# A state-space recurrence whose decay products move from GpSimd to VectorE

## The chip, the cores and the metric

The kernel runs on one core of a Trainium2 chip, as one launch. A core has a matrix engine (TensorE, "PE" in the profile, with its weight loads as "PEld"), VectorE ("DVE"), ScalarE ("ACT"), GpSimd ("POOL") and SyncE ("SP"), each with an instruction queue of its own that runs in order. They share the on-chip memory SBUF. TensorE writes to PSUM, here used as eight banks of 128x512 float32. The metric is the device time of one execution in microseconds (us), the median of several runs.

## The reference, cut to what matters

Two transformer-like blocks run one after the other on 512 tokens of width 1024. The second block has three branches, and one of them is a state-space model (16 heads of width 64, state size 128) that is scanned forward and backward over the sequence in chunks of 128 positions. What is computed per chunk is this:

```python
def ssd_scan(xh, dt, a_coef, bm, cm, h0, want_y):
    ...
    xdt = (xh.astype(f32) * dt[..., None]).reshape(b, nc, q, G, hg, P)
    acs = jnp.cumsum((dt * a_coef.astype(f32)).reshape(b, nc, q, G, hg), axis=2)
    decay_end = jnp.exp(acs[:, :, -1:] - acs)
    states = jnp.einsum('bcjgn,bcjghp->bcghpn', bc, xdt * decay_end[..., None])
    chunk_decay = jnp.exp(acs[:, :, -1])
    def step(h, inp):
        st, dec = inp
        return h * dec[..., None, None] + st, h
    ...
    lmat = jnp.exp(jnp.where(tri[:, :, None, None], seg, -jnp.inf))
    cb = jnp.einsum('bcign,bcjgn->bcijg', cc, bc)
    y_diag = jnp.einsum('bcijgh,bcjghp->bcighp', cb[..., None] * lmat, xdt)
    y_off = jnp.einsum('bcign,bcghpn->bcighp', cc, h_in) * jnp.exp(acs)[..., None]
```

The change touches `cb[..., None] * lmat`, the product of the C-B scores (one 128x128 matrix for each of two groups of heads) with the decays (one 128x128 matrix for each of 16 heads).

## The kernel before

The kernel is written out for each engine by hand: one function per engine and stage, with semaphores between them and no scheduler. The order of the calls is the order of each engine's queue.

The recurrence is `pe_ssm`, `dve_ssm`, `act_ssm` and `pool_ssm`. `ssm_units()` lists twelve chunks: two of the context, then four of the sequence, forward; then two of the context and four of the sequence, backward. The eight chunks of the sequence (`OWN_UNITS`) also yield output; they are called chunk 1 to chunk 8 here, 1 to 4 forward and 5 to 8 backward. Between chunk 4 and chunk 5 lie the two backward context chunks, which only update the state.

What each engine does for one of chunks 1 to 8, in the order of its queue:

- **TensorE**: the old state's part of the output (C times state, two banks, after `ssm_h`); the state's update (B times `xw`, two banks, after `ssm_x`); for the next chunk the C-B scores (one bank) and four banks of decay sums, in `pe_ssm_decays`; then for each of the two groups, after `ssm_probs`, eight heads' products of probabilities (in `decay`) with `xdt`, one bank each. Chunk 8 has no next chunk. Behind it stands `pe_ssm_out`, a projection of 128 matmul records that needs nothing from the recurrence but its turn in the queue.
- **VectorE**: `xw` and `xdt` (128x1024 each, through the helper `tt`, whose operations all carry line 2687); then `ssm_x`; the old state's part scaled (L2715), in the backward direction with an added sum into y (another L2687); the state times its decay (L2687) and plus its update (L2727), for both groups; `ssm_h`; the C-B scores of the next chunk, masked into `cb` (L2665, `dve_ssm_cb`); and the two sums of the group outputs into y (L2737), each followed by `ssm_y`.
- **ScalarE**: for each group, 8 activations on the decay sums (L2791) and one exponential over 128x1024 (L2795), into one of three buffers `decay`. The buffer of three groups earlier must be free (`ssm_y`). Then it raises `ssm_exp`.
- **GpSimd**: for each group, after `ssm_exp` and (once a chunk) `ssm_cb`, the product of the decays with the scores, 128x1024, in place (L2775); then `ssm_probs`.

`decay` has two buffers in the tensor `scratch` and the third in `slots_of_units`. `cb` has two buffers. `to_dve` rotates over four PSUM banks, which VectorE must free, and `to_act` over four others.

Of the kernel before, what the change touches and what calls it, by code (L numbers as in the profile page):

```python
# [10 lines left out]
ALU = mybir.AluOpType  # L11
# [3 lines left out]
P = 128  # L15
# [264 lines left out]
def build(nc, a, table, where, out):  # L280

    ctx = ExitStack()
    with ctx:
# [3 lines left out]
        def sem(name):  # L287
            return ctx.enter_context(nc.semaphore(name))

        def signal(name):  # L290
            return Signal(sem(name))
# [30 lines left out]
        def part(at, *shape):  # L322

            n = int(np.prod(shape))
            assert at + n <= SCRATCH, (at, shape)
            v = scratch[:, at:at + n]
            if len(shape) == 2:
                v = v.rearrange("p (a b) -> p a b", b=shape[1])
            if len(shape) == 3:
                v = v.rearrange("p (a b c) -> p a b c", b=shape[1], c=shape[2])  # L330
            return v

        def con(name, width=None):
            at, n = where[name]
            return const[:, at:at + (width or n)]
# [25 lines left out]
        dve_done = sem("dve_done")  # L361
        pool_done = sem("pool_done")
# [2017 lines left out]
        decay = [*(part(SSM_TMP + i * 1024, 8, P) for i in range(2)), sel.rearrange("p a t s -> p (a t) s")]  # L2380
        cb = [part(SSM_TMP + 2048, 2, P), part(SSM_TMP + 4864, 2, P)]
# [10 lines left out]
        xs_ready = signal("xs_ready")  # L2392
        ssm_x = signal("ssm_x")
        acs_turned = signal("acs_turned")
        ssm_cb = signal("ssm_cb")
        ssm_y = signal("ssm_y")
        ssm_exp = signal("ssm_exp")
        ssm_probs = signal("ssm_probs")
# [206 lines left out]
        OWN_UNITS = [(d, c) for d, c in ssm_units() if c < TT]  # L2605
# [56 lines left out]
        def dve_ssm_cb(dve, i):  # L2662
            dve.wait_ge(to_dve.full, to_dve.next_full())
            bank = to_dve.take()
            dve.tensor_tensor(cb[i % 2], bank[:, 0:256].rearrange("p (g i) -> p g i", g=2),  # L2665
                              con("upper" if OWN_UNITS[i][0] == 0 else "lower").rearrange("p (g i) -> p g i", g=1)
                              .broadcast_to([P, 2, P]), ALU.mult).then_inc(to_dve.free, 1)
            dve.wait_ge(to_dve.free, to_dve.own_reads())
            dve.sem_inc(ssm_cb.sem, 1)

        def dve_acs_rows(dve, step):
            dve.tensor_copy(acs_own, acs[:, :, 0:64]).then_inc(dve_done, 1)
# [13 lines left out]
        def dve_ssm(dve, step):  # L2686
# [3 lines left out]
            n_own = 0  # L2690
# [4 lines left out]
            for d, c in ssm_units():  # L2695
                own = c < TT
                xs = heads(xs_tok[:, c, :] if own else ctx_xs[:, c - TT, :])
                tt(heads(xw), xs, over(head_cols(w_end, d, c), SSM_P), ALU.mult).then_inc(dve_done, 1)
                dve.wait_ge(dve_done, step.next())
                if own:  # L2700
                    tt(heads(xdt), xs, over(head_cols(d_t, d, c), SSM_P), ALU.mult).then_inc(dve_done, 1)
                    dve.wait_ge(dve_done, step.next())
                dve.sem_inc(ssm_x.sem, 1)
                y_g = lambda g: y_tok[:, c, g * 512:(g + 1) * 512].rearrange("p (h x) -> p h x", x=SSM_P)
                if own:
                    if n_own == 0:
                        dve_ssm_cb(dve, 0)
                    n_own += 1
                    if c == (0 if d == 0 else TT - 1):
                        dve.sem_inc(ssm_h.sem, 1)  # L2710
                    for g in range(2):
                        dve.wait_ge(to_dve.full, to_dve.next_full())
                        bank = to_dve.take()
                        dst = y_g(g) if d == 0 else y_part.rearrange("p (h x) -> p h x", x=SSM_P)
                        dve.tensor_tensor(dst, bank[:, :].rearrange("p (h x) -> p h x", x=SSM_P),  # L2715
                                          over(head_cols(e_acs, d, c, g), SSM_P), ALU.mult).then_inc(to_dve.free, 1)
                        dve.wait_ge(to_dve.free, to_dve.own_reads())
                        if d == 1:
                            tt(y_g(g), y_g(g), dst, ALU.add).then_inc(dve_done, 1)
                            dve.wait_ge(dve_done, step.next())  # L2720
                for g in range(2):
                    h = h_state[d][:, 8 * g:8 * g + 8, :]
                    tt(h, h, over(head_cols(e_tot, d, c, g), SSM_P), ALU.mult).then_inc(dve_done, 1)
                    dve.wait_ge(dve_done, step.next())
                    dve.wait_ge(to_dve.full, to_dve.next_full())
                    bank = to_dve.take()
                    dve.tensor_tensor(h, h, bank[:, :].rearrange("p (h x) -> p h x", x=SSM_P), ALU.add).then_inc(to_dve.free, 1)  # L2727
                    dve.wait_ge(to_dve.free, to_dve.own_reads())
                if own:
                    if c != (TT - 1 if d == 0 else 0):  # L2730
                        dve.sem_inc(ssm_h.sem, 1)
                    if n_own < len(OWN_UNITS):
                        dve_ssm_cb(dve, n_own)
                    for g in range(2):
                        dve.wait_ge(to_dve.full, to_dve.next_full())
                        bank = to_dve.take()
                        dve.tensor_tensor(y_g(g), y_g(g), bank[:, :].rearrange("p (h x) -> p h x", x=SSM_P), ALU.add)\  # L2737
                           .then_inc(to_dve.free, 1)
                        dve.wait_ge(to_dve.free, to_dve.own_reads())
                        dve.sem_inc(ssm_y.sem, 1)  # L2740
# [25 lines left out]
        y_rms = part(SSM_TMP + 2048, TT)  # L2766
        ys_t = freed[0].rearrange("p (m t) -> p m t", t=T)

        def pool_ssm(pool, step):
            for i in range(len(OWN_UNITS)):  # L2770
                pool.wait_ge(ssm_cb.sem, ssm_cb.next(pool))
                for g in range(2):
                    own = decay[(2 * i + g) % 3]
                    pool.wait_ge(ssm_exp.sem, ssm_exp.next(pool))
                    pool.tensor_tensor(own, own, cb[i % 2][:, g:g + 1, :].broadcast_to([P, 8, P]), ALU.mult)\  # L2775
                        .then_inc(pool_done, 1)
                    pool.wait_ge(pool_done, step.next())
                    pool.sem_inc(ssm_probs.sem, 1)

        def act_ssm(act, step):  # L2780
            for i, (d, c) in enumerate(OWN_UNITS):
# [630 lines left out]
        @block.gpsimd  # L3412
        def _(pool):
            step = Order()
            pool_s5_steps(pool)
            pool_row_loads(pool)
            pool_s5_loads(pool)
            pool_s5(pool, step)
            pool_moe_loads(pool)
            pool_bias(pool, step)  # L3420
            pool_store_tokens(pool)
            pool_moe(pool, step)
            pool_ssm(pool, step)
            pool_rope_load(pool)

        @block.tensor
# [117 lines left out]
```

## Time and profile before

| | us |
|---|---|
| median of 3 runs | 3664.16 |
| lowest and highest | 3656.54, 3665.57 |
| the profiled execution | 3668.7 |
| its span, first to last instruction | 3666.9 |
| TensorE busy in the span | 3200.5 (87%) |
| VectorE busy | 1231.0 (34%) |
| ScalarE busy | 521.5 (14%) |
| GpSimd busy | 269.6 (7%) |

The eight chunks of the recurrence run from about 2209.7 us to 2326 us of the span. Times in the rows count from the start of the span. A row of the timeline gives the start, the duration of the merged instructions, engine, source line, what is written and read, how many instructions were merged, and in brackets the engine's idle time before them and what ended it. A merged row shows the shape of its first instruction. A float32 matmul into a bank leaves two records, so that two banks show as x4.

### The profile page before, as it was taken

Reading aid. Unit: us, or ns where it says so; the run is one execution under the profiler, and the core shown is the slowest. Engines: PE = TensorE matmul, PEld = TensorE weight load, DVE = VectorE, ACT = ScalarE, POOL = GpSimd, SP = SyncE. Lnnn points to the kernel's source line nnn. Section 1 sums busy time; section 2 is a strip of 40 time slices with the busy share of each in tenths; the row PEclk is TensorE's granted clock in tenths of the full one; section 3 lists DMA queues with packets and bytes.
Section 4 is the critical chain, followed back from the end, with each engine's and each line's share of the span. In section 5 each row is a group of like instructions: output and inputs, shape, how many; then the busy total and the mean of one; then the engine's idle time right before and its main releaser. Section 6 shows DMA issues by size and latency. Waiting matters only on the chain.

```text
span 3666.9 us, 33500 instructions
## 1 busy us (share of the span) xinstructions
PE 3200.5 (87%) x13492; PEld 1532.1 (42%) x13493; DVE 1231.0 (34%) x2047; ACT 521.5 (14%) x981; POOL 269.6 (7%) x352
## 2 busy tenths in 40 slices
PE   4894758699999999999994888978868999899998
PEld 2352223444443333333332554446636444344444
DVE  3126990523223232323233236514254001212201
ACT  1211001200110000000001214213133000100000
POOL 0005650200000000000000003100000000000000
PEclk8896779699999999999997798986879999999999
DMA  9511410289999999999993110010000222121210
GB/s 294 179 69 55 149 69 23 88 321 330 327 334 333 356 352 360 352 355 353 359 360 134 46 35 1 24 52 1 24 23 1 69 81 92 46 90 59 75 63 23
DMA packets 287682, 582.43 MB, mean 159 GB/s; under 512 B 7953, under 2 KB 12492, under 8 KB 287500
## 3 DMA queue, kind: packets, MB, share of 16 engines
q1 hardware_dynamic: 281184, 561.20, 42.7%
q0 software_dynamic: 5072, 15.80, 1.9%
q10 hardware_dynamic: 1276, 3.29, 0.2%
q8 instruction: 110, 1.80, 0.2%
q14 instruction: 40, 0.33, 0.0%
HBM read 576.08 MB, written 4.19 MB: 158 GB/s over the span
## 4 chain that ended last, share of the span: by engine, by line
PE 77%; DVE 15%; ACT 3%; issue 2%; SPq 1%; POOL 1%; DMA 1%; ACTq 1%; DVEq 0%; PEldq 0%; POOLq 0%
PE psum_all L211 74%; DVE scratch L1197 4%; PE psum_all L219 3%; DVE hidden L2039 2%; SPq L188 1%; DVE scratch L1221 1%; DVE scratch L3102 1%; DVE scratch L2687 1%; ACTq L566 1%; DVE scratch L1214 1%; ACT scratch L3164 1%; DMA panel<-in_ada_w 1%; DVE scratch L2983 1%; ACT hidden L424 0%; DVE scratch L832 0%
## 5 line engine op out<-in xcount | busy, mean ns | idle before, releaser
L211 PE MATMUL psum_all<-panel,scratch 128*64 128x512 f32 (+3 forms) x5568 | 977.5, 507 | 1.4 <-ACTq L1814 0.8
L211 PE MATMUL psum_all<-hidden,panel 128*128 128x512 f32 (+1 forms) x1808 | 795.2, 601 | 31.3 <-ACT hidden L424 20.9
L211 PEld LDWEIGHTS psum_all<-hidden,panel 128*128 128x128 f32 (+1 forms) x1808 | 346.5, 192 | 471.3 <-issue 440.9
L211 PEld LDWEIGHTS psum_all<-panel,scratch 128*64 128x64 f32 (+2 forms) x5568 | 333.8, 131 | 472.7 <-issue 426.1
L211 PE MATMUL psum_all<-scratch 128*128 128x64 f32 (+8 forms) x1512 | 371.3, 442 | 132.5 <-DVEq L1235 82.5
L211 PEld LDWEIGHTS psum_all<-scratch 128*128 128x128 f32 (+2 forms) x1512 | 232.6, 235 | 242.5 <-DVEq L1235 97.9
L2039 DVE TENSOR_TENSOR hidden<-hidden,psum_all 128x512 f32<-128x512 f32 x264 | 169.6, 684 | 290.9 <-PE psum_all L211 290.9
L211 PE MATMUL psum_all<-scratch,panel 128*128 128x512 f32 (+1 forms) x672 | 250.5, 531 | 2.0 <-DVE resid L3289 1.0
L219 PE MATMUL psum_all<-const,scratch 128*128 128x128 f32 (+4 forms) x954 | 152.2, 299 | 114.4 <-DMA scratch<-in_s_lambda_im 32.9
L219 PEld LDWEIGHTS psum_all<-const,scratch 128*128 128x128 f32 (+4 forms) x954 | 111.0, 157 | 215.1 <-issue 109.5
L211 PE MATMUL psum_all<-scratch,const 128*128 128x512 f32 (+5 forms) x308 | 120.0, 534 | 83.1 <-ACT scratch L415 32.1
L211 PEld LDWEIGHTS psum_all<-scratch,panel 128*128 128x128 f32 x672 | 127.5, 190 | 127.5 <-issue 119.6
L2029 DVE SCALAR_TENSOR_TENSOR y_low<-psum_all,scratch,y_high 128x512 fp32r<-128x512 f32 (+1 forms) x49 | 33.6, 686 | 271.5 <-ACT y_high L2001 271.5
L211 PE MATMUL psum_all<-tokens_r,y_high 64*128 64x512 f32 (+2 forms) x360 | 97.0, 496 | 28.2 <-DVE hidden L2039 26.6
L211 PE MATMUL psum_all<-panel,hidden 128*128 128x512 f32 (+2 forms) x384 | 111.4, 455 | 10.4 <-ACT hidden L424 10.4
L211 PEld LDWEIGHTS psum_all<-scratch,const 128*128 128x128 f32 x308 | 59.0, 234 | 135.2 <-issue 68.2
L1812 ACT ACTIVATE scratch<-psum_all 128x512 f32<-128x512 f32 (+1 forms) x49 | 26.7, 545 | 617.8 <-PE psum_all L219 617.8
L1425 POOL DMA_INDIRECT scratch<-token_rows,scratch x33 | 30.8, 934 | 1115.5 <-DVEq L1771 1115.5
L211 PE MATMUL psum_all<-panel 128*128 128x512 f32 x256 | 110.5, 592 | 1.7 <-DVEq L3280 1.7
L1197 DVE TENSOR_TENSOR scratch<-scratch 128x512 f32<-128x512 f32 x128 | 104.9, 840 | 4.6
L2019 DVE TENSOR_SCALAR scratch<-psum_all 128x512 f32<-128x512 f32 (+1 forms) x49 | 30.7, 626 | 218.6 <-PE psum_all L211 218.6
L2539 DVE TENSOR_SCALAR scratch<-psum_all,cols 128x512 f32<-128x512 f32 (+1 forms) x44 | 33.0, 750 | 193.2 <-PE psum_all L211 193.2
(323 smaller groups left out, 2299.8 us busy)
## 6 DMA issues: line engine op xcount, KB each, us to landing
panel<-in_exp_w_gu SPq DMA_DIRECT2D x132, 2048.0 KB, 11.8
panel<-in_exp_w_down SPq DMA_DIRECT2D x66, 2048.0 KB, 14.3
panel<-in_w_in SPq DMA_DIRECT2D x17, 2048.0 KB, 8.3
panel<-in_ada_w SPq DMA_DIRECT2D x12, 2048.0 KB, 20.1
panel<-in_w_mod SPq DMA_DIRECT2D x12, 2048.0 KB, 7.9
panel<-in_ffn_w_gate SPq DMA_DIRECT2D x5, 2048.0 KB, 7.8
panel<-in_ffn_w_up SPq DMA_DIRECT2D x5, 2048.0 KB, 7.7
panel<-in_w_out SPq DMA_DIRECT2D x4, 2048.0 KB, 7.8
```

The source lines that it names most:

```text
L188: sp.dma_start(dst, src.rearrange("(k p) c -> p k c", p=P)).then_inc(self.loaded[s], 16)
L211: ins = self.pe.matmul(out, lhsT, rhs, start=start, stop=stop)
L219: return self.pe.transpose(out, in_, ident)
L566: act.dma_start(rows[at:at + n, tile_no, :], flat(name).rearrange("(r c) -> r c", c=P))\
L1197: tt = lambda o, x, y, op: dve.tensor_tensor(o, x, y, op)
L1214: dve.tensor_tensor_scan(z_re, mag, w1, 0.0, ALU.mult, ALU.add).then_inc(dve_done, 1)
L1221: dve.tensor_tensor_scan(z_im, mag, w3, 0.0, ALU.mult, ALU.add).then_inc(dve_done, 1)
L2039: dve.tensor_tensor(hidden[:, m, :], hidden[:, m, :], moe_y(no)[:, :], ALU.add).then_inc(shares_free, 1)
L2687: tt = lambda o, x, y, op: dve.tensor_tensor(o, x, y, op)
L2983: dve.reciprocal(nrm_std[:, 0:n], nrm_std[:, 0:n]).then_inc(dve_done, 1)
L3102: dve.tensor_reduce(tmp_max[:, 0:1], pair[:, 512 - w:768], AX_X, ALU.max).then_inc(dve_done, 1)
L3164: act.activation(p_sb[u % 2][:, 0:w + CTX], att_pairs[u % 2][:, 512 - w:768], ACT.Exp, bias=neg_max[n % 2][:, h:h + 1], scale=HD ** -0.5, ...
```

## The change

The function `pool_ssm` and its call are gone, with the semaphore `ssm_cb`. A function `dve_ssm_probs` makes the same two products on VectorE. `dve_ssm` calls it in each of chunks 1 to 8 behind the state's updates and `ssm_h`, ahead of `dve_ssm_cb` for the next chunk and ahead of the two sums into y.

```diff
@@
-        ssm_cb = signal("ssm_cb")
@@
             dve.wait_ge(to_dve.free, to_dve.own_reads())
-            dve.sem_inc(ssm_cb.sem, 1)
@@
                     if c != (TT - 1 if d == 0 else 0):
                         dve.sem_inc(ssm_h.sem, 1)
+                    dve_ssm_probs(dve, step, n_own - 1)
                     if n_own < len(OWN_UNITS):
                         dve_ssm_cb(dve, n_own)
@@
-        def pool_ssm(pool, step):
-            for i in range(len(OWN_UNITS)):
-                pool.wait_ge(ssm_cb.sem, ssm_cb.next(pool))
-                for g in range(2):
-                    own = decay[(2 * i + g) % 3]
-                    pool.wait_ge(ssm_exp.sem, ssm_exp.next(pool))
-                    pool.tensor_tensor(own, own, cb[i % 2][:, g:g + 1, :].broadcast_to([P, 8, P]), ALU.mult)\
-                        .then_inc(pool_done, 1)
-                    pool.wait_ge(pool_done, step.next())
-                    pool.sem_inc(ssm_probs.sem, 1)
+        def dve_ssm_probs(dve, step, i):
+            for g in range(2):
+                own = decay[(2 * i + g) % 3]
+                dve.wait_ge(ssm_exp.sem, ssm_exp.next(dve))
+                dve.tensor_tensor(own, own, cb[i % 2][:, g:g + 1, :].broadcast_to([P, 8, P]), ALU.mult).then_inc(dve_done, 1)
+                dve.wait_ge(dve_done, step.next())
+                dve.sem_inc(ssm_probs.sem, 1)
@@
-            pool_ssm(pool, step)
```

VectorE's queue in chunk 3 (forward), before. The lines are those named above, from `xw` and `xdt` to the two sums into y:

```order
L2687 TENSOR_TENSOR scratch<-panel,scratch 128x1024 x2
L2715 TENSOR_TENSOR panel<-psum_all,scratch 128x512 x2
L2687 TENSOR_TENSOR scratch<-scratch 128x512
L2727 TENSOR_TENSOR scratch<-scratch,psum_all 128x512
L2687 TENSOR_TENSOR scratch<-scratch 128x512
L2727 TENSOR_TENSOR scratch<-scratch,psum_all 128x512
L2665 TENSOR_TENSOR scratch<-psum_all,const 128x256
L2737 TENSOR_TENSOR panel<-panel,psum_all 128x512 x2
```

The same place after the change. Line numbers there are one or two lower, and the products stand at L2772:

```order
L2685 TENSOR_TENSOR scratch<-panel,scratch 128x1024 x2
L2713 TENSOR_TENSOR panel<-psum_all,scratch 128x512 x2
L2685 TENSOR_TENSOR scratch<-scratch 128x512
L2725 TENSOR_TENSOR scratch<-scratch,psum_all 128x512
L2685 TENSOR_TENSOR scratch<-scratch 128x512
L2725 TENSOR_TENSOR scratch<-scratch,psum_all 128x512
L2772 TENSOR_TENSOR scratch<-scratch 128x1024
L2772 TENSOR_TENSOR slots_of_units<-slots_of_units,scratch 128x1024
L2664 TENSOR_TENSOR scratch<-psum_all,const 128x256
L2736 TENSOR_TENSOR panel<-panel,psum_all 128x512 x2
```

Two operations of 128x1024 now stand between the last state update and the next chunk's scores.

VectorE's queue in chunk 8, the last (backward), after the change, from the state's decays and updates on; before, the two rows of L2772 were absent and the rest was the same:

```order
L2685 TENSOR_TENSOR scratch<-scratch 128x512
L2725 TENSOR_TENSOR scratch<-scratch,psum_all 128x512
L2685 TENSOR_TENSOR scratch<-scratch 128x512
L2725 TENSOR_TENSOR scratch<-scratch,psum_all 128x512
L2772 TENSOR_TENSOR slots_of_units<-slots_of_units,scratch 128x1024
L2772 TENSOR_TENSOR scratch<-scratch 128x1024
L2736 TENSOR_TENSOR panel<-panel,psum_all 128x512 x2
L2685 TENSOR_TENSOR panel<-panel,row_vectors 128x1024
```

Nothing moved on TensorE. Its queue in chunk 8 and behind it, with its waits, is the same before and after: old state, update, the two groups behind `ssm_probs`, and the projection:

```order
L211 MATMUL psum_all<-scratch 128x512 [waits dve_banks_free,ssm_h]
L211 MATMUL psum_all<-scratch 128x512 [waits dve_banks_free]
L211 MATMUL psum_all<-scratch 128x512 [waits dve_banks_free,ssm_x]
L211 MATMUL psum_all<-scratch 128x512 [waits dve_banks_free]
L211 MATMUL psum_all<-scratch,slots_of_units 128x64 [waits dve_banks_free,ssm_probs]
L211 MATMUL psum_all<-scratch,slots_of_units 128x64 x7
L211 MATMUL psum_all<-scratch 128x64 [waits dve_banks_free,ssm_probs]
L211 MATMUL psum_all<-scratch 128x64 x7
L211 MATMUL psum_all<-panel,hidden 128x512 [waits act_banks_free,panel2_0_loaded]
```

What moved is who raises `ssm_probs` for the two waits there: GpSimd before, VectorE after its state updates now.

## Rows read from the trace of the kernel before

**Rows 1.** The page: busy us (share of the span of 3666.9 us) by engine.

```profile
PE 3200.5 (87%) x13492; PEld 1532.1 (42%) x13493; DVE 1231.0 (34%) x2047; ACT 521.5 (14%) x981; POOL 269.6 (7%) x352
```

**Rows 2.** The chain that ended last (start, us, what), around chunks 6 and 7.

```profile
2294.99 9.39 PE psum_all L211 x48
...
2307.84 9.39 PE psum_all L211 x48
```

**Rows 3.** The same chain from chunk 8 on.

```profile
2320.69 60.50 PE psum_all L211 x164
```

**Rows 4.** GpSimd's products in `scratch`, by line: duration ns min/median/max, first and last start.

```profile
L2775 POOL TENSOR_TENSOR scratch<-scratch x11: 2349/2361/3155, 2214.9 to 2319.7; 128x1024 f32<-128x1024 f32 x11
```

**Rows 5.** VectorE by line and shape, 2195 to 2332 us: busy us, mean ns | idle before.

```profile
L2687 DVE TENSOR_TENSOR scratch<-scratch 128x512 f32<-128x512 f32 x24 | 22.1, 919 | 1.3
L2687 DVE TENSOR_TENSOR scratch<-panel,scratch 128x1024 f32<-128x1024 f32 x16 | 19.6, 1225 | 1.2
...
L2687 DVE TENSOR_TENSOR panel<-panel,scratch 128x512 f32<-128x512 f32 x8 | 9.1, 1140 | 0.3
```

**Rows 6.** Timeline of VectorE in chunk 3, forward.

```profile
2237.76 2.48 DVE L2687 TENSOR_TENSOR scratch<-panel,scratch 128x1024 f32<-128x1024 f32 x2
...
2241.84 1.16 DVE L2687 TENSOR_TENSOR scratch<-scratch 128x512 f32<-128x512 f32 x1
...
2244.49 0.69 DVE L2727 TENSOR_TENSOR scratch<-scratch,psum_all 128x512 f32<-128x512 f32 x1
2245.32 0.42 DVE L2665 TENSOR_TENSOR scratch<-psum_all,const 128x256 f32<-128x256 f32 x1
```

**Rows 7.** Timeline of TensorE in chunk 3.

```profile
2240.36 2.43 PE L211 MATMUL psum_all<-scratch 128*128 128x512 f32 x8 [1.70 <-DVEq L2703]
...
2246.06 1.89 PE L211 MATMUL psum_all<-scratch 128*128 128x64 f32 x16
```

**Rows 8.** Timeline of GpSimd: a product in chunk 3, one in the context chunks.

```profile
2239.30 3.15 POOL L2775 TENSOR_TENSOR slots_of_units<-slots_of_units,scratch 128x1024 f32<-128x1024 f32 x1 [2.60 <-ACTq L2797]
...
2265.01 2.72 POOL L2775 TENSOR_TENSOR scratch<-scratch 128x1024 f32<-128x1024 f32 x1 [2.59 <-ACTq L2797]
```

**Rows 9.** Timeline of VectorE in chunk 6, backward.

```profile
2295.75 1.89 DVE L2687 TENSOR_TENSOR panel<-panel,scratch 128x512 f32<-128x512 f32 x1
...
2301.29 0.69 DVE L2727 TENSOR_TENSOR scratch<-scratch,psum_all 128x512 f32<-128x512 f32 x1
```

**Rows 10.** Timeline of TensorE in chunk 6, the first group's products.

```profile
2300.69 1.90 PE L211 MATMUL psum_all<-scratch 128*128 128x64 f32 x16
```

**Rows 11.** Timeline of VectorE in the first backward context chunk.

```profile
2266.76 1.52 DVE L2687 TENSOR_TENSOR scratch<-scratch 128x512 f32<-128x512 f32 x1
```

**Rows 12.** Timeline of VectorE in chunk 8.

```profile
2321.45 1.88 DVE L2687 TENSOR_TENSOR panel<-panel,scratch 128x512 f32<-128x512 f32 x1
...
2326.99 0.69 DVE L2727 TENSOR_TENSOR scratch<-scratch,psum_all 128x512 f32<-128x512 f32 x1
```

**Rows 13.** Timeline of TensorE: chunk 8's first group, then the projection behind it.

```profile
2322.51 1.90 PE L211 MATMUL psum_all<-scratch,slots_of_units 128*128 128x64 f32 x16
...
2326.03 55.15 PE L211 MATMUL psum_all<-panel,hidden 128*128 128x512 f32 x128
```

**Rows 14.** Timeline of TensorE behind two of its idle stretches.

```profile
2270.37 2.08 PE L211 MATMUL psum_all<-scratch 128*128 128x512 f32 x2 [3.59 <-DVEq L2703]
...
2403.66 8.86 PE L211 MATMUL psum_all<-hidden,panel 128*128 128x512 f32 x13 [5.67 <-issue]
```

**Rows 15.** Stretches: length, PE, PEld, DVE, ACT, POOL busy, PE clock, DMA, GB/s.

```profile
2270.00:2273.00 3.00, 2.63 (x3) 1.18 (x4) 1.40 (x3) 0.00 (x0) 0.00 (x0) 0.50 0.00 0
2273.00:2276.00 3.00, 0.77 (x2) 0.00 (x0) 2.86 (x5) 0.00 (x0) 0.00 (x0) 0.96 0.01 3
...
2405.00:2408.00 3.00, 3.00 (x4) 1.01 (x3) 0.00 (x0) 0.00 (x0) 0.00 (x0) 0.50 0.00 0
2408.00:2411.00 3.00, 3.00 (x6) 1.26 (x5) 0.00 (x0) 0.00 (x0) 0.00 (x0) 0.70 0.00 0
```

## Prediction, written before the change was run

> **What bounds the kernel now.** I read the page first, then the chain that ended last, then the timelines of the engines in the recurrence. The page shows TensorE busy 87% of a span of 3666.9 us, VectorE 34% and GpSimd 7% [rows 1], but these are averages over many stages, and the change touches about 117 us of them. The chain shows what ends last there. In chunk 6 it is an unbroken 9.39 us of TensorE, the next chunk's begins 12.85 us later, and the 3.46 us between are VectorE: the second sum into y, then xw and xdt [rows 2]. From chunk 8 on the chain stays on TensorE for 60.50 us, through the projection behind the recurrence [rows 3]. GpSimd is on the chain nowhere in the stage: a product takes it 2.35 to 3.16 us [rows 4], but it is done before TensorE asks for it. So the question isn't whether VectorE makes the product faster. It is whether VectorE gets to it before TensorE does, since it now stands behind VectorE's own state updates.
>
> **What a product costs on VectorE.** The trace has no product of decays and scores on VectorE. The nearest rows are xw and xdt: same size of 128x1024 float32, two SBUF inputs, one of them broadcast, 1.23 us each [rows 5]. The other end is what GpSimd needs for the very same operands, 2.36 us [rows 4]. I take 1.24 us, because the engine, the size and the kind of operands agree, and keep 2.36 for the range. Nothing in the shape suggests less than 1.23.
>
> **What goes away.** The sixteen products leave GpSimd, about 40 us of it; by itself that is worth nothing, as it is off the chain. But some of VectorE's operations get shorter. An operation of 128x512 on two SBUF inputs takes 0.69 us when it is left alone, and 1.16 us in chunk 3 [rows 6], 1.89 in chunk 6 [rows 9], 1.52 in the context chunk [rows 11]. Each long one ends 0.55 us after a GpSimd product ends: 2243.00 against 2242.45, and 2268.28 against 2267.73 [rows 6, 8, 11]. So it had stood waiting for that product. Over the stage this makes 22.1 - 24 x 0.69 = 5.5 us and 9.1 - 8 x 0.69 = 3.6 us, 9.1 us together [rows 5]. The Trainium skill has this as a rule (SBUF — State Buffer, section Who interferes with whom): a VectorE instruction with two SBUF inputs and a GpSimd instruction that reads SBUF exclude one another, and the later one waits out the first. The trace agrees. With the change these waits end, and the question is where on the chain they lay.
>
> **Forward chunks.** In chunk 3 the last state update ends at 2244.49 + 0.69 = 2245.18 [rows 6]. Without the wait (1.16 - 0.69 = 0.47) it ends at 2244.71. From such an end to the next operation behind a semaphore is 0.14 us (2245.18 to 2245.32 [rows 6]), then the product's 1.24, and from the end of xdt to TensorE's start is 0.12 us (2240.24 to 2240.36 [rows 6, 7]). TensorE can begin the first group at 2244.71 + 0.14 + 1.24 + 0.12 = 2246.21. Before, it began at 2246.06 [rows 7]. So 0.15 us is lost. The second product is ready 1.4 us later, and TensorE is busy with the first group for 1.9 us, so it costs nothing. The scores for the next chunk (L2665) and the sums into y queue behind the products; the scores' bank is needed only by the next chunk's old-state matmul, which waits for the second group anyway, and the sums wait for TensorE. Chunks 2, 3 and 4 have the same pattern: 3 x 0.15 = 0.45 us. In chunks 1 and 5 TensorE does the old state's matmuls behind xw instead of ahead of it, and so asks for the first group later; the same working puts the first product ready 0.3 and 0.8 us ahead of need there: nothing.
>
> **Context chunk.** The wait in the first backward context chunk lies on the chain, which is VectorE there: 1.52 - 0.69 = 0.83 us gained [rows 11].
>
> **Backward chunks 6 and 7.** VectorE has two more sums into y ahead of the state updates. The last update ended at 2301.98, and without the wait (1.89 - 0.69 = 1.20) at 2300.78 [rows 9]. Plus 0.14 + 1.24 + 0.12 gives 2302.28, against 2300.69 before [rows 10]: 1.59 us each, 3.2 for two. Had the wait not gone it would be 2.79 each.
>
> **Chunk 8.** Here TensorE has no work for a next chunk, so it wants the first group 3.4 us earlier relative to VectorE, at 2322.51 [rows 13]. VectorE's last update ended at 2327.68, without the wait (1.88 - 0.69) at 2326.49 [rows 12]. Plus 0.14 + 1.24 + 0.12: 2327.99, so 5.5 us lost. Nothing hides this: the projection's 128 records stand behind these groups in TensorE's queue, run at 55.15 us without a pause [rows 13], and the chain goes through them [rows 3]. VectorE's own tail behind chunk 8 moves too, but it runs beside that projection.
>
> **TensorE's clock.** This stall is a TensorE idle of about 5.3 us, and there is none so long in the stage before. After an idle of 3.59 us the granted clock was 0.50, that is 1.2 GHz, and back up by about 2273.2: some 2.9 us of work at the lower level [rows 14, 15]. After an idle of 5.67 us it was at 0.50 until about 2409.8 (0.70 over 2408 to 2411), 6.1 us of work [rows 14, 15]. Work at 1.2 GHz loses half its time: 1.4 and 3.1 us, and 0 if the clock holds. I take 2.3 us, the middle of the two that were seen. The context chunks pass through such a fall before as well; with 0.83 us less idle there it may come out up to 1.4 us better, which I leave to the range.
>
> **The sum.** 0.45 - 0.83 + 3.2 + 5.5 + 2.3 = 10.6 us. Against the profiled execution, 3668.7 us, that is 3679.3. That execution lies 4.5 us above the median of 3664.16, and the runs span 3656.54 to 3665.57, so the sum goes onto the median: 3674.8 us, +0.29%. A measurement of this kernel can tell about 0.3%, 11 us, from no change; the forecast lies just inside that.
>
> **The rivals.**
> - **The clock gives way more often** (slower). In chunks 6 and 7 TensorE gets a second idle of 1.5 us beside the 1.70 us that it has (as in [rows 7]). If the clock falls in each of them as it did after 5.67 us, that is 2 x 3.1 = 6.2 us more: 3681. It decides from the point where two short idles count as one long; against it, the clock stays up in these chunks before.
> - **The product is slow on VectorE** (slower). At 2.36 us, each first product is 1.12 later, on the path in chunks 2, 3, 4, 6, 7, 8, and partly in 1 and 5 (6 x 1.12 + 0.8 + 0.3 = 7.8); the second product then comes 2.5 us after the first, 0.8 more than TensorE's group lasts, 8 x 0.8 = 6.4. Together 14.2: 3689. Against it stand the 1.23 us of like operations.
> - **The last stall is taken back** (same). If what follows chunk 8 were waiting for something else, a panel or ScalarE, the 5.5 + 2.3 would vanish: 3667. Against it, the chain is TensorE alone for 60.50 us.
> - **The lifted waits win** (faster). This is the rule of the skill carried to its end. If all 9.1 us that VectorE stood waiting came off the path, and the products were covered, as GpSimd's were: 3664.2 - 9.1 = 3655. Against it, only 0.83 us of them lie on the chain before; the rest serve to bring the products forward.
>
> **How the numbers follow.** The forecast gets 0.53, and its variant without the clock's fall (3672.5) 0.14; the clock rival 0.12, the slow product 0.06, the absorbed stall 0.10, the lifted waits 0.05. The forecast lies next to the bound of 0.3%, and a median of few runs moves by some us, so it gives 0.27 to slower and 0.26 to same; its variant 0.12 to same and 0.02 to slower. Slower: 0.27 + 0.02 + 0.11 + 0.06 = 0.46. Same: 0.26 + 0.12 + 0.01 + 0.10 + 0.02 = 0.51. Faster: 0.03. The range runs from 3665, just under the absorbed stall, to 3684, past the clock rival with the runs' scatter. It leaves out the slow product and the lifted waits.
>
> **What would show it.** In the profile of the changed kernel: VectorE's products at 1.24 us; no VectorE operation of 128x512 above 0.7 us in the stage; chunks 2 to 4 a period of 13.0 us, chunks 6 and 7 one of 14.4 (12.85 before); TensorE idle about 5.3 us ahead of chunk 8's first group, with `ssm_probs` as what ends it, and a granted clock of 0.50 behind. If the exponentials rather than the products ended a wait, if the period stayed at 12.85 in chunks 6 and 7, or if the projection still began within 1 us of its old distance to chunk 8's xdt, the reasoning would be wrong.

## The result, and the profile after

The changed kernel took 3674.21 us in the median of 9 runs (3670.46 to 3677.91), against 3665.54 us of the kernel before in 9 runs. The ratio is 1.0024, with a 95% interval of 1.0014 to 1.0035: slower by 8.7 us, next to the forecast of 3674.8, and inside what was to be called no change (0.3%). Run again beside the experiments it came out at 3678.09 against 3667.29, 1.0035 (1.0022 to 1.0047), just outside; both intervals hold 0.3%. The size lies between 0.24% and 0.35%, as far as is known.

The page of the kernel after, busy time by engine, answers [rows 1]:

```profile
PE 3200.6 (87%) x13492; PEld 1531.3 (42%) x13493; DVE 1241.6 (34%) x2063; ACT 521.6 (14%) x981; POOL 226.8 (6%) x336
```

GpSimd lost 16 instructions and 42.8 us. VectorE gained 16 and only 10.6 us, since 19.6 us of products came in and some 9 us of waiting went out. The products by line (duration ns min/median/max, first and last start) answer [rows 4]:

```profile
L2772 DVE TENSOR_TENSOR scratch<-scratch x11: 1225/1225/1227, 2217.7 to 2330.6; 128x1024 f32<-128x1024 f32 x11
L2772 DVE TENSOR_TENSOR slots_of_units<-slots_of_units,scratch x5: 1224/1225/1226, 2230.9 to 2329.2; 128x1024 f32<-128x1024 f32 x5
```

All sixteen took what xw takes, 1.23 us, half of GpSimd's 2.36.

VectorE's timeline in chunk 3 of the kernel after answers [rows 6]: the operation that had taken 1.16 us takes 0.69, and the two products stand behind the last state update, 0.15 us after it.

```profile
2241.01 0.69 DVE L2685 TENSOR_TENSOR scratch<-scratch 128x512 f32<-128x512 f32 x1
...
2243.18 0.69 DVE L2725 TENSOR_TENSOR scratch<-scratch,psum_all 128x512 f32<-128x512 f32 x1
2244.02 1.23 DVE L2772 TENSOR_TENSOR scratch<-scratch 128x1024 f32<-128x1024 f32 x1
2245.39 1.23 DVE L2772 TENSOR_TENSOR slots_of_units<-slots_of_units,scratch 128x1024 f32<-128x1024 f32 x1
```

TensorE's timeline in chunks 6, 7 and 8 of the kernel after answers [rows 10, 13]. The first three rows begin with a first group, and the bracket names VectorE's signal behind the product (line 2774) as what TensorE waited for. The last two are chunk 8's second group and the projection, whose row ends with the window shown:

```profile
2300.10 2.00 PE L211 MATMUL psum_all<-scratch 128*128 128x64 f32 x16 [1.41 <-DVEq L2774]
...
2314.64 10.77 PE L211 MATMUL psum_all<-scratch 128*128 128x64 f32 x40 [1.42 <-DVEq L2774]
2330.53 3.67 PE L211 MATMUL psum_all<-scratch,slots_of_units 128*128 128x64 f32 x16 [5.13 <-DVEq L2774]
2334.00 3.62 PE L211 MATMUL psum_all<-scratch 128*128 128x64 f32 x16
2337.41 7.80 PE L211 MATMUL psum_all<-panel,hidden 128*128 128x512 f32 x14
```

The stalls are near those of the forecast (1.5 and 5.3): 1.4 us in chunks 6 and 7, 5.1 in chunk 8. But the groups of chunk 8 took 3.67 and 3.62 us instead of 1.90 each [rows 13], at half the clock. The stretches of 3 us of the kernel after (columns as in [rows 15]) show the clock down in chunk 7 and again behind chunk 8's stall, where it had stood at 1.00 before:

```profile
2316.00:2319.00 3.00, 3.00 (x19) 3.00 (x19) 1.11 (x2) 1.47 (x6) 0.00 (x0) 0.61 0.00 0
2319.00:2322.00 3.00, 3.00 (x8) 1.81 (x8) 1.91 (x2) 2.87 (x5) 0.00 (x0) 0.50 0.00 0
...
2331.00:2334.00 3.00, 3.00 (x17) 3.00 (x16) 0.79 (x1) 0.00 (x0) 0.00 (x0) 0.50 0.00 0
...
2337.00:2340.00 3.00, 3.00 (x6) 1.53 (x7) 2.16 (x3) 0.00 (x0) 0.00 (x0) 0.50 0.00 0
2340.00:2343.00 3.00, 3.00 (x8) 1.38 (x7) 2.93 (x3) 0.00 (x0) 0.00 (x0) 0.90 0.00 0
```

From chunk 1's xw to the end of the projection the kernel before took 171.5 us and the one after 185.4: 13.9 us more, while the whole grew by 8.7 in the median and the span of the profiled execution by 5.9. Chunk 1's xw began 1.0 us earlier (2208.72 against 2209.68), in code that nobody touched; over all traces it lies between 2206.8 and 2211.5. The rest of the difference is behind the projection. The chain of the kernel after, start and duration of three pieces: the first attention's input projection, the second's, and the feed-forward's first long piece.

```profile
2416.55 51.71 PE psum_all L211 x192
...
2621.04 49.99 PE psum_all L211 x192
2835.94 276.41 PE psum_all L211 x640
```

The same of the kernel before:

```profile
2403.66 51.80 PE psum_all L211 x192
...
2612.16 49.79 PE psum_all L211 x192
2830.00 276.44 PE psum_all L211 x640
```

The first attention took 204.5 us after and 208.5 before, the second 214.9 and 217.8. Neither was touched. From the feed-forward to the end it is 836.9 us in both.

The 2.9 us of the second attention have one place. It repeats a group of 20 matmul records, which take 2.83 us at almost every place in both chains; only the one that starts 195 us into this attention differs. First the kernel before, then the kernel after:

```profile
2807.03 5.37 PE psum_all L211 x20
```

```profile
2815.51 2.83 PE psum_all L211 x20
```

Over 2808 to 2811 us the granted clock was 0.50 in the kernel before, and in the kernel after it was 1.00 over 2815 to 2818. So the kernel before had a fall of the clock there that the kernel after did not have.

### The profile page after: what moved, and what is told of

Same layout as the page of the kernel before. It is cut to its first block, busy times and chain, and to the rows that moved or that the text cites. A ratio compares the mean times of both kernels' runs of the same rounds, so it can differ in the third digit from the quotient of the medians.

```text
span 3672.8 us, 33491 instructions
## 1 busy us (share of the span) xinstructions
PE 3200.6 (87%) x13492; PEld 1531.3 (42%) x13493; DVE 1241.6 (34%) x2063; ACT 521.6 (14%) x981; POOL 226.8 (6%) x336
## 4 chain that ended last, share of the span: by engine, by line
PE 76%; DVE 15%; ACT 3%; issue 2%; SPq 1%; POOL 1%; ACTq 1%; DMA 1%; DVEq 0%; PEldq 0%; POOLq 0%
PE psum_all L211 73%; DVE scratch L1197 4%; PE psum_all L219 3%; DVE hidden L2039 2%; SPq L188 1%; DVE scratch L1221 1%; DVE scratch L2685 1%; DVE scratch L3098 1%; ACTq L566 1%; DVE scratch L1214 1%; ACT scratch L3160 1%; DMA panel<-in_ada_w 1%; DVE scratch L2979 1%; ACT hidden L424 0%; DVE scratch L832 0%
## 5 line engine op out<-in xcount | busy, mean ns | idle before, releaser
L211 PE MATMUL psum_all<-panel,hidden 128*128 128x512 f32 (+2 forms) x384 | 112.9, 459 | 10.4 <-ACT hidden L424 10.4
```

The costliest lines, as they stand in the source:

```text
L211: ins = self.pe.matmul(out, lhsT, rhs, start=start, stop=stop)
```

## The experiments

The table reads every trace at the same places. "Stage" is chunk 1's xw to the end of the projection; "6 and 7" are the periods from xw to xw of these chunks; the attention columns go from each input projection's start to the next of the three pieces above. All in us of one profiled execution; the last two columns are the median and the ratio to the kernel before, timed beside it, with its interval. The medians were taken in four rounds, in which the kernel before had 3665.54 (before and after), 3667.29 (e1 to e4), 3665.99 (e5 to e8) and 3666.26 us (e9 to e12), so kernels of different rounds are compared by their ratios. In e7 and e8 xw stands elsewhere in the queue, and no period is given.

| kernel | stage | 6 and 7 | attention 1, 2 | median | ratio |
|---|---|---|---|---|---|
| before | 171.5 | 12.85, 12.85 | 208.5, 217.8 | 3665.54 | |
| after | 185.4 | 14.53, 16.01 | 204.5, 214.9 | 3674.21 | 1.0024 (1.0014 to 1.0035) |
| e1, after again | 185.4 | 14.53, 15.99 | 197.9, 214.8 | 3678.09 | 1.0035 (1.0022 to 1.0047) |
| e2, chunk 8 on GpSimd | 183.2 | 16.72, 16.43 | 204.6, 219.9 | 3680.1 | 1.0036 (1.0024 to 1.0048) |
| e3, only chunk 8 on VectorE | 181.9 | 12.85, 12.85 | 208.2, 214.8 | 3674.7 | 1.0023 (1.0014 to 1.0031) |
| e4, chunk 8's idle filled | 180.6 | 14.53, 16.00 | 209.0, 214.9 | 3678.62 | 1.0028 (1.0016 to 1.0039) |
| e5, products early | 185.2 | 14.65, 14.67 | 204.6, 215.0 | 3677.57 | 1.0032 (1.0020 to 1.0045) |
| e6, no product | 169.4 | 12.85, 12.85 | 206.9, 217.7 | 3666.42 | 1.0001 (0.9992 to 1.0010) |
| e7, xw ahead, GpSimd | 181.1 | | 212.0, 214.9 | 3675.94 | 1.0024 (1.0015 to 1.0033) |
| e8, xw ahead, VectorE | 177.8 | | 205.0, 215.0 | 3669.6 | 1.0011 (1.0002 to 1.0020) |
| e9, later by one | 171.5 | 12.86, 12.85 | 204.1, 217.6 | 3663.64 | 0.9996 (0.9987 to 1.0005) |
| e10, later by two | 171.5 | 12.85, 12.85 | 206.7, 217.7 | 3669.61 | 1.0007 (0.9998 to 1.0016) |
| e11, all idle filled | 179.2 | 14.54, 14.53 | 207.3, 215.0 | 3673.95 | 1.0018 (1.0009 to 1.0027) |
| e12, decays ahead | 169.6 | 14.31, 14.31 | 207.0, 217.6 | 3664.59 | 0.9996 (0.9987 to 1.0005) |

**The changed kernel again.** No edit.

> The changed kernel once more, as the yardstick for the runs beside it, and to see whether the stretches that the change does not touch keep their length. In its trace the stretch from chunk 1's xw to the end of the projection grew by 13.9 us, while the whole grew by about 8.7 us in the median. Theory: the stalls are fixed (1.5 us in chunks 6 and 7, 5.1 in chunk 8), and the rest is TensorE's clock, which falls at other moments from run to run; so the same stalls here, another total by up to some 5 us, and 3674 us in the median. Rival: the attention stages behind really became 7 us shorter by the change; then they are 7 us shorter than before here too.

The stage was the same to 0.1 us, with the same falls of the clock, as the theory has it; the median came out 4 us above the expected 3674. The rival isn't decided: the second attention took 214.8 us again, 3.0 less than before, but the first moves by more than that between the two executions. The first attention took 197.9 us instead of 204.5, with the same instructions: these two executions of one kernel differ by 6.6 us there, as the chain of this one shows.

```profile
2417.18 51.75 PE psum_all L211 x192
...
2615.06 49.94 PE psum_all L211 x192
2829.87 276.40 PE psum_all L211 x640
```

So a total read from single executions says little. The stage's own length was the same in both.

**Chunk 8 on GpSimd.** The edit is made on the kernel before: `pool_ssm` stays, for the chunks that are not listed in `ON_VECTOR`, and counts the signals of the listed ones without waiting for them (excerpt).

```diff
+                    if n_own - 1 in ON_VECTOR and n_own - 1 not in EARLY:
+                        dve_ssm_probs(dve, step, n_own - 1)
...
+        ON_VECTOR, EARLY = (0, 1, 2, 3, 4, 5, 6), ()
...
             for i in range(len(OWN_UNITS)):
+                if i in ON_VECTOR:
+                    ssm_cb.next(pool)
+                    ssm_exp.next(pool, 2)
+                    continue
```

> The change is undone for chunk 8 alone: VectorE makes the products of chunks 1 to 7, GpSimd the two of chunk 8. Theory (the position behind the state updates costs where TensorE has nothing else to do): chunk 8 is as before, its xw to the projection's start takes 7.9 us instead of 16.6, and of the 8.7 us that were lost only 0.45 - 0.83 + 3.2 = 2.8 us stay: 3665.5 + 2.8 = 3668 us, up to 1.5 more where the clock falls in chunk 7. Rival (the clock gives way wherever TensorE idles a little more, whatever chunk 8 does): 3671 or more. Rival (the product on VectorE is what costs, evenly over the chunks): 7/8 of the loss stays, 3673.

It came out at 3680, not 3668. The theory missed and its first rival, that the clock gives way whatever chunk 8 does, held. TensorE's timeline of this kernel shows the 1.4 us stalls of chunks 6 and 7, and behind the first a second group at half speed (3.62 us) and the old state's matmuls (3.08 us):

```profile
2302.47 2.57 PE L211 MATMUL psum_all<-scratch 128*128 128x64 f32 x16 [1.41 <-DVEq L2780]
2304.83 3.62 PE L211 MATMUL psum_all<-scratch,slots_of_units 128*128 128x64 f32 x16
2308.25 3.08 PE L211 MATMUL psum_all<-scratch 128*128 128x512 f32 x4
```

The clock fell in chunk 6 and in chunk 7, which cost 2.2 and 1.9 us beyond the 14.53 that the stalls alone give, and again in chunk 8, where TensorE's longest idle stretch is now 2.4 us. The stage is 11.7 us longer than before, against 13.9: taking away the largest stall left most of the loss. Up to chunk 7 this kernel makes the same products in the same places as the changed one, but its clock isn't the same. Here it stood at 0.50 from about 2266.2 to 2283.2 us without a break, through the context chunks and into chunk 5; in the kernel after it was down for 6.8 and 3.4 us there, with 1.00 between. TensorE's idle ahead of the first context chunk was 2.56 us here and 2.21 there. That this is why the clock fell in chunk 6 here and not there was not tested.

**Only chunk 8 on VectorE.** The same code with `ON_VECTOR, EARLY = (7,), ()`.

> The other half: GpSimd makes the products of chunks 1 to 7 and VectorE only the two of chunk 8. Theory: chunk 8's stall of 5.1 to 5.5 us is there in full, with a clock loss behind it of 2.3 (as forecast) to 5.0 us (as the changed kernel's trace has it): 3665.5 + 7.5 to 10.5 = 3673 to 3676 us, and chunks 2 to 7 at a period of 12.85 us. Rival (evenly over the chunks): 3667 us.

This one hit: 3674.7 us, chunks 6 and 7 at 12.85, and chunk 8 as in the kernel after. The stage grew by 10.4 us, of which the stall from xw to the first group is 5.3 and the clock 5.0:

```profile
2327.43 3.67 PE L211 MATMUL psum_all<-scratch,slots_of_units 128*128 128x64 f32 x16 [5.18 <-DVEq L2780]
2330.90 3.62 PE L211 MATMUL psum_all<-scratch 128*128 128x64 f32 x16
```

Chunk 8 alone costs 0.23%, the other seven alone 0.36%, and all eight 0.24 to 0.35%. In the stage it is 10.4 us, 11.7 and 13.9. The parts don't add up. The stalls are the same 1.4, 1.4 and 5.2 us, but e2 has a longer fall of the clock from the context chunks on and one in chunk 6 that the kernel after doesn't have.

**Chunk 8's idle filled.** TensorE runs five matmuls into the bank that the first group overwrites.

```diff
+                        if n_own == len(OWN_UNITS) and g == 0:
+                            pe.wait_ge(to_dve.free, to_dve.room())
+                            for _ in range(5):
+                                mm(to_dve.banks[to_dve.at_write % 4][:, :], ident, hidden[:, 0, :])
                         pe.wait_ge(ssm_probs.sem, ssm_probs.next(pe))
```

> The changed kernel, and TensorE runs five matmuls of 128x512 (ten records, 4.3 us at 2.4 GHz) in chunk 8's idle stretch, into the bank that the first group overwrites; the stall itself stays. Theory: the clock stays at 2.4 GHz through the two groups and the projection's start, so the loss of about 5.0 us behind the stall (3.4 in the groups, 1.6 in the projection) is gone: 3674 - 5 = 3669 us, with ssm_probs still awaited. Rival (the stall is the loss, and the clock would have come up at once): 3674 us, no change.

In the stage the theory held: 180.6 us, 4.8 less than the kernel after. In the total it can't be seen: 3678.62, where 3669 was expected; beside the kernel after's 3678.09, timed in the same round, it is no gain. Why stays open; the first attention took 209.0 us in this execution and 204.5 and 197.9 in the two of the kernel after, which is more than the gain.

**All idle filled.** The same, with one matmul in chunks 6 and 7 as well (excerpt).

```diff
+                        if n_own >= 6 and g == 0:
...
+                            for _ in range(5 if n_own == len(OWN_UNITS) else 1):
```

> The changed kernel, with TensorE's idle stretches filled in chunk 6 and chunk 7 (one matmul of 128x512 each, 0.86 us of 1.4) as well as in chunk 8 (five). Theory (the short stalls of chunks 6 and 7 bring the clock down in chunk 7, as its trace shows for 6.8 us): the clock stays at 2.4 GHz through chunks 6 to 8, and the stretch from chunk 1 to the end of the projection is 171.5 + 8.3 = 180 us, against 185.4 in the changed kernel's trace. In the total that is 3674 to 3678 less 5 us, if the attention behind does not give it back. Rival (the falls come from something else): the clock falls in chunk 7 all the same.

The clock stayed at 1.00 through chunks 6 to 8. Its timeline of TensorE has the stalls (0.9 us left of chunk 8's, behind the fill), and groups of 2.00 and 1.95 us:

```profile
2327.38 2.00 PE L211 MATMUL psum_all<-scratch,slots_of_units 128*128 128x64 f32 x16 [0.90 <-DVEq L2778]
2329.21 1.95 PE L211 MATMUL psum_all<-scratch 128*128 128x64 f32 x16
```

The stage took 179.2 us (180 was expected), 6.2 less than the kernel after. VectorE's products come as late as in the kernel after: in chunk 8 the first group starts 9.8 us behind xw in both. So of the 13.9 us, 7.7 are stalls less what was gained ahead of them, and 6.2 are what the clock took in chunks 7 and 8. In the total, 1.0018 is below both ratios of the kernel after, though the intervals overlap.

**Products early.** All on VectorE, in chunks 2 to 8 right behind xw and xdt (excerpt; `EARLY` lists these chunks).

```diff
+                    if n_own - 1 in EARLY:
+                        dve_ssm_probs(dve, step, n_own - 1)
                     for g in range(2):
                         dve.wait_ge(to_dve.full, to_dve.next_full())
```

> All products on VectorE, but in chunks 2 to 8 right behind xw and xdt, ahead of the old state's part and the state updates; chunk 1 as in the change. Theory (where they stand in VectorE's queue costs, not that VectorE makes them): no stall ahead of chunk 8's first group, since the product is ready at 2320.6 + 0.14 + 1.24 + 0.12 = 2322.1 against 2322.5 when TensorE wants it; forward chunks at 12.85 us; in chunks 6 and 7 VectorE's own work adds up to about 13.4 us a chunk (10.3 + 2.6 of products + gaps), so 0.5 us each. Sum -0.8 + 2 x 0.5 = about 0 against before: 3665.5 us. Rival (VectorE's load itself is what costs): the time of the changed kernel, 3674.

Missed: 3677.57, forward chunks at 14.66 us. The stall had moved. TensorE's timeline in chunk 3 of this kernel:

```profile
2241.84 1.98 PE L211 MATMUL psum_all<-scratch 128*128 128x512 f32 x4 [1.70 <-DVEq L2703]
2245.36 0.71 PE L211 MATMUL psum_all<-scratch 128*128 128x128 f32 x4 [1.54 <-DVE panel L2717]
```

The matmul that waits 1.54 us is the next chunk's C-B scores. It needs the bank of the old state's part, which VectorE frees (here line 2717) behind the products. With four banks for seven fills a chunk, VectorE's early operations are awaited too. I had looked only at when the product was ready. In chunk 8 the first group waited 1.63 us for a bank in the same way, and the clock fell behind it. The total is nearer to the rival's, but VectorE's load is not what bounds the forward chunks: in chunk 3 it idles 1.78 and 1.10 us ahead of its two sums, waiting for TensorE. What this run leaves standing of the theory is that the place in the queue decides; that an early place costs nothing was wrong.

**No product.** GpSimd passes the semaphores on and multiplies nothing.

```diff
-                    own = decay[(2 * i + g) % 3]
                     pool.wait_ge(ssm_exp.sem, ssm_exp.next(pool))
-                    pool.tensor_tensor(own, own, cb[i % 2][:, g:g + 1, :].broadcast_to([P, 8, P]), ALU.mult)\
-                        .then_inc(pool_done, 1)
-                    pool.wait_ge(pool_done, step.next())
```

> The kernel before without the products: nobody multiplies the decays by the scores (the output lacks that factor), GpSimd only passes the semaphores on. This measures what GpSimd's products cost VectorE before. Theory: all waits of VectorE's operations vanish (9.1 us busy time), but only 0.83 us of them lie on the chain: 3664.7 us, chunk periods at 12.85. Rival (the waits were on the path): 3656 us.

As the theory has it: 1.0001. In the total, GpSimd's products and all the waiting that they caused on VectorE were worth nothing that can be measured. The stage was 2.1 us shorter: 0.8 us from chunk 4's xw to chunk 5's, and 1.3 in chunk 5, where the clock came back earlier. The rival of the lifted waits is out.

**xw ahead of the sums.** On the kernel before and on the changed one (excerpt).

```diff
+                    if k + 1 < len(units):
+                        dve_xw(*units[k + 1])
+                        ahead = True
                     for g in range(2):
                         dve.wait_ge(to_dve.full, to_dve.next_full())
```

> The kernel before, products on GpSimd, but VectorE makes the next chunk's xw behind the scores and ahead of the two sums into y, in time in which it idles (2.25 + 1.10 us in a forward chunk); xdt follows the sums and has a semaphore of its own that TensorE awaits ahead of the groups. Theory: TensorE's idle of 1.70 us ahead of the state's matmuls vanishes in chunks 2 to 4 and the two context chunks behind them, and about 0.9 us of it in each of the backward chunks, where VectorE fills up: 5 x 1.7 + 3 x 0.9 = about 11 us, at least 7: 3655 to 3659 us. Rival (VectorE then becomes the bound in all chunks because xw delays the sums into y): 3665 us or more.

> The same edit on the changed kernel, so that the products stay on VectorE, behind the state updates. Theory: VectorE is now the bound in the backward chunks and its queue is all that TensorE waits for; in forward chunks it adds up to 2.5 + 1.4 + 2.8 + 2.7 + 0.6 + 1.4 = 11.4 us of work, so they still gain some 1.0 to 1.5 us each; chunks 6 and 7 gain about 1 us, chunk 8's stall shrinks only where xw was ahead, by 1.2 us. Altogether 4 to 7 us below the changed kernel: 3667 to 3670 us, and 10 us above the version with GpSimd. Rival (products on VectorE and xw ahead cover each other, GpSimd is not needed): within 2 us of that version.

With GpSimd it lost: 3675.94, forward chunks at 13.5 us. TensorE no longer waits 1.70 us for xw, but 1.1 us for a bank behind a sum into y, and 1.0 for the scores' bank. That is the rival's side, and 17 us above the expected 3655 to 3659. With VectorE's products it gained: 3669.6, within the expected 3667 to 3670, and 1.0011, against 1.0024 and 1.0035 of the changed kernel. The interval (1.0002 to 1.0020) overlaps the first of these and not the second. The order between the two was the reverse of what I expected.

**The attention later.** GpSimd writes the rotation table with zeros once or twice ahead of its load.

```diff
+            for _ in range(1):
+                pool.memset(rope.rearrange("p a t -> p (a t)"), 0.0).then_inc(pool_done, 1)
+                pool.wait_ge(pool_done, step.next())
```

> The kernel before, and GpSimd sets the rotation table's 1024 columns to zero once more ahead of the load on which the attention behind the recurrence waits, so that the attention begins later by one such operation, about 1 to 1.3 us, and nothing else is touched. Theory (the attention stages lose more or less to TensorE's clock depending on when they start, so that time lost in the recurrence is not passed on one for one): the stretch from the attention's start to the feed-forward's start, 426.3 us in the trace before and 412.7 to 426.9 in the nine others, is not the same here as before, and the total moves by something else than the delay, anywhere from -4 to +5 us. Rival (a shift is a shift): the stretch stays, the total grows by the delay, 1.0003.

> The same with two such operations, a delay of 2 to 2.6 us. Theory: again not the delay; and if the attention's own clock is what decides, the stretch behind it differs from that with one. Rival: the total grows by 2.0 to 2.6 us, 1.0006.

The gap ahead of the attention grew by 0.9 and 2.0 us. The medians moved by -2.6 and +3.4 us, and both intervals hold 1 and the plain delay. On the total this is inconclusive. The second attention kept its 217.6 and 217.7 us.

**Decays ahead.** TensorE's `pe_ssm_decays` ahead of the state's matmuls, VectorE's `dve_ssm_cb` ahead of the updates, products on GpSimd (excerpt; both calls are removed from their old places).

```diff
+                if own and n_own < len(OWN_UNITS):
+                    pe_ssm_decays(pe, mm, OWN_UNITS[n_own])
                 pe.wait_ge(ssm_x.sem, ssm_x.next(pe))
...
+                if own and n_own < len(OWN_UNITS):
+                    dve_ssm_cb(dve, n_own)
```

> The kernel before (products on GpSimd), with TensorE's scores and decay sums for the next chunk moved ahead of the state's matmuls, and VectorE's masking of the scores ahead of the state updates. TensorE then has 4.1 us of work while VectorE makes xw and xdt, where it idled 1.70 us a chunk, and no bank is asked for earlier than it is free (the old state's bank is still held when the move of xw was tried). Theory: chunks 2 to 4 at a period of 11.2 us instead of 12.85, chunks 6 and 7 at 11.5 to 12; 3 x 1.65 + 2 x 1.0 = 7 us less in the stage, more if chunk 5 gains too, and 3659 us in the total, if the attention behind keeps its length. Rival (VectorE, which has 10.3 us of work a chunk and waits for GpSimd's products besides, is the bound): periods of 12.5 us and more, no measurable gain.

Forward chunks fell to 11.2 and 11.4 us, as expected. Chunks 6 and 7, expected at 11.5 to 12, rose to 14.31. The stage is 1.9 us shorter, where 7 were expected, and the total, 0.9996, is no change. VectorE's timeline of this kernel in chunk 6 tells why; both long ones are again operations with two SBUF inputs beside a GpSimd product:

```profile
2290.24 2.03 DVE L2687 TENSOR_TENSOR panel<-panel,scratch 128x512 f32<-128x512 f32 x1
...
2294.32 2.88 DVE L2687 TENSOR_TENSOR scratch<-scratch 128x512 f32<-128x512 f32 x1
```

The two GpSimd products beside them end at 2291.72 and 2296.67 us, 0.55 and 0.53 us ahead of the ends of these operations. Here the exclusion costs: 1.3 and 2.2 us a chunk on an engine that had become the bound, since VectorE idles nowhere in that chunk. So the rival, that VectorE is the bound, held in the backward chunks and the theory in the forward ones. No version tried beats the kernel before beyond the uncertainty.

## Why the prediction was right, point by point

- **What a product costs.** 1.24 us, measured 1.225. Right, and its other end of 2.36 was not needed.
- **Forward chunks.** 0.15 us each, measured 0.22, 0.23 and 0.13 (periods and chunk 4's end). TensorE began when I said, 8.42 us behind xw in chunk 3 (8.45 forecast, 8.30 before). What I left out is the first group itself: behind the wait it took 2.00 us instead of 1.89, in chunks 2, 3, 5 and 6 alike.
- **Context chunks.** A gain of 0.83, measured 0.73.
- **Chunks 1 and 5.** Nothing, measured -0.09 and -0.96. The latter is clock: it fell ahead of chunk 5 and stayed at 0.50 for 6.8 us before and for 3.4 us after. This is the gain of up to 1.4 us that I had left to the range. As TensorE was sooner done with its earlier work, my 0.8 us of cover had turned into a wait of 0.34 us.
- **Chunks 6 and 7.** 1.59 us each; chunk 6 measured 1.68. Chunk 7 measured 3.16, since the clock fell there for about 1.5 us more. That was the first rival, given 0.12, and it came in part: in one of the two chunks here, in both in e2, in neither in e3, which has no stalls there, and in neither in e5, which has stalls of 1.70 and 1.54 us in each. So two short idles are not enough to say that the clock falls.
- **Chunk 8.** 5.5 us, measured 5.34 from xw to the first group (9.76 against 4.42). Nothing hid it. By the rows TensorE wants this group 3.9 us earlier relative to xw than in chunk 7 (4.42 against 8.30), not the 3.4 that I gave; the sum didn't use that figure.
- **The clock behind chunk 8.** This is the term that was mis-sized: 2.3 us, measured 5.0 (3.4 in the groups, 1.6 in the projection); e11 puts all of the clock, chunk 7's with it, at 6.2. I took the middle of two recoveries, 2.9 and 6.1 us of work long, and overlooked a third in the same stage: ahead of chunk 5, behind an idle of 3.64 us, the clock fell, and came back only at 2283.5 us, 6.1 us into the work. This one lasted 10.1 us of work, from 2330.5 to 2340.6 us, so even the longest seen before would have given 3.1 and not 5.0. Why it lasted longer the runs don't show.
- **What I left out.** The sum for the stage was 10.6, measured 13.9. The total came out at +8.7 and +10.8 in two sets, and in the profiled execution the stages behind gave back 6.9 us, 4.0 in the first attention and 2.9 in the second. The first scatters too much to tell, from 197.9 to 212.0 us over all traces. The second took 214.8 to 215.0 us in eight of the nine traces whose stage was longer than 177 us (219.9 in the other, e2), and 217.6 to 217.8 in all five with a stage under 172. The fall of the clock shown above separates them: the group 195 us in took 5.3 to 5.4 us in those five and in e2, and 2.8 in the eight. So 2.9 us came back in a stage that nobody touched, as one fall less. What decides whether it falls there was not shown. It isn't the start in the span alone, since e8's second attention began at 2613.29 us and took 215.0, e10's at 2614.11 and took 217.7, and e1's at 2615.06 and took 214.8. The forecast of 3674.8 was so near by luck in part: the stage's miss of 3.3 us and this return, which no term of the sum foresaw, nearly cancel.

## What to carry to other kernels

Moving work to a faster engine is worth what the slower one cost on the path, and here that was 2.1 us of a stage and nothing measurable in the total (e6), while the price is set by where the work lands in the new queue and by who waits behind it, for data or for a bank. Look for the place where the waiting engine has no other work, here the last chunk, and add to the stall what the clock takes behind it. Where a stage passes through several falls of the clock, read its stalls and its clock apart in the trace, and don't expect parts of an edit to add up in the total.

## What the runs showed of the hardware that I had not expected

- Behind chunk 8's stall TensorE was busy without a pause for 6.9 us of 64-column matmuls at a granted clock of 0.50, and came back to 1.00 only 3.2 us into the 512-column matmuls of the projection, 10.1 us in all. In e3, behind a stall of 5.18 us, it was 10.2 us. That is why the term was too small.
- Idles of 1.70 and 1.42 us in one chunk went with a fall of the clock in chunk 7 of the kernel after and not in its chunk 6; in e2 it fell in chunk 6 with the same two, and in chunk 7 with 0.60 and 1.42. In e5 1.70 and 1.54 us a chunk left it at 1.00 in chunks 6 and 7. The length of the idles alone doesn't tell. One matmul that took 0.86 us of each stall kept it up (e11).
- One fall of the clock late in the second attention, 5.37 us against 2.83 for the same 20 records, was there in six of the 14 traces, and its code was the same in all.
- Two executions of the same kernel with the same stage differed by 6.6 us in one attention stage.
